# The selective scan of a hybrid decoder: running sums of the decays made once and spread through memory, one state without padding, outputs gathered chunk by chunk

## The reference

```python
a = dt * A                                  # per token and head, 32 heads in 8 groups of 4
a_cs = cumsum(a, within chunks of 128)      # 4 chunks
seg = a_cs[l] - a_cs[s]
Lmat = exp(where(l >= s, seg, -inf))
CB = C @ B.T                                # per group and chunk
y_diag = (CB * Lmat) @ X                    # X = x * dt, 64 features a head
chunk_states = B.T @ (exp(a_cs[-1] - a_cs) * X)
state = state * exp(a_cs[-1]) + chunk_states    # from chunk to chunk
y_off = (C @ state) * exp(a_cs)
y = (y_diag + y_off + d_skip * x) * silu(z)
y = y * rsqrt(mean(y * y within the group's 256 features) + eps) * norm_w
out = y @ w_out
```

## Time and profile before

| | us |
|---|---|
| median of 3 runs | 2250.75 (2249.43 to 2251.53) |
| the profiled execution | 2249.22 |
| its span | 2247.3 |
| TensorE busy in it | 2152.0 |
| VectorE busy | 1235.4 |
| ScalarE busy | 848.4 |

### The profile page before, as it was taken

One profiled execution on the slowest core, in us unless ns is written; L12 is line 12 of the kernel. 1 busy time (PEld: TensorE's weight loads), 2 busy tenths in 40 slices (PEclk: granted clock), 3 DMA queues, 4 the chain that ended last, 5 costly groups with the idle time before them and its releaser, 6 DMA issues. The chain is left out here.

```text
span 2247.3 us, 28900 instructions
## 1 busy us (share of the span) xinstructions
PE 2152.0 (96%) x10542; PEld 1807.0 (80%) x10542; DVE 1235.4 (55%) x2024; ACT 848.4 (38%) x1235; POOL 9.2 (0%) x30
## 2 busy tenths in 40 slices
PE   4999999899999999899999989999998899999998
PEld 2888888788888878788888878888887778888887
DVE  6555466778887763655556653333345765333323
ACT  4333322554445542422222344443134645322212
POOL 0000000000000000000000000000010000000000
PEclk8999999999999999999999999999999999999999
DMA  7555576112211113455547522223322012223231
GB/s 296 202 191 194 176 249 236 63 57 85 66 65 65 57 57 106 150 186 199 199 173 251 181 75 93 93 93 103 113 94 66 1 47 85 93 93 101 96 112 66
DMA packets 77528, 276.80 MB, mean 123 GB/s; under 512 B 8592, under 2 KB 11152, under 8 KB 77328
## 3 DMA queue, kind: packets, MB, share of 16 engines
q1 hardware_dynamic: 77456, 275.81, 35.7%
HBM read 273.68 MB, written 2.10 MB: 123 GB/s over the span
## 5 line engine op out<-in xcount | busy, mean ns | idle before, releaser
L236 PE MATMUL bank<-h_hi,w_hi_sb 128*128 128x512 f32 (+1 forms) x1984 | 757.6, 382 | 41.4 <-DVE h_lo L369 27.6
L237 PE MATMUL bank<-h_lo,w_hi_sb 128*128 128x512 f32 (+1 forms) x1984 | 749.0, 378 | 0.0
L238 PE MATMUL bank<-h_hi,w_lo_sb 128*128 128x512 f32 (+1 forms) x1984 | 748.5, 377 | 0.0
L231 DVE TENSOR_TENSOR w_lo_sb<-raw,w_hi_sb 128x1024 fp32r<-128x1024 f32 x356 | 419.9, 1197 | 124.9 <-ACT w_hi_sb L226 120.7
L236 PEld LDWEIGHTS bank<-h_hi,w_hi_sb 128*128 128x128 f32 x1984 | 376.1, 190 | 119.5 <-issue 21.5
L237 PEld LDWEIGHTS bank<-h_lo,w_hi_sb 128*128 128x128 f32 x1984 | 376.3, 190 | 69.0 <-issue 1.7
L238 PEld LDWEIGHTS bank<-h_hi,w_lo_sb 128*128 128x128 f32 x1984 | 376.1, 190 | 68.5
L226 ACT ACTIVATE w_hi_sb<-raw 128x1024 fp32r<-128x1024 f32 x356 | 352.7, 1031 | 86.7 <-PE bank L238 85.9
L236 PE MATMUL bank<-a_hi,w_hi_sb 128*128 128x512 f32 (+1 forms) x792 | 290.1, 366 | 0.0
L237 PE MATMUL bank<-a_lo,w_hi_sb 128*128 128x512 f32 (+1 forms) x792 | 289.4, 365 | 0.0
L238 PE MATMUL bank<-a_hi,w_lo_sb 128*128 128x512 f32 (+1 forms) x792 | 289.4, 365 | 0.0
(11 more groups left out here) (200 smaller groups left out, 1880.7 us busy)
## 6 DMA issues: line engine op xcount, KB each, us to landing
raw<-w_stream SPq DMA_DIRECT2D x356, 512.0 KB, 4.4
mod_raw<-w_mod SPq DMA_DIRECT2D x144, 512.0 KB, 4.4
first_mod<-w_mod SPq DMA_DIRECT2D x16, 512.0 KB, 14.5
x_trunk<-x_in SPq DMA_DIRECT2D x1, 2048.0 KB, 10.5
trunk_out<-x_trunk SPq DMA_DIRECT2D x2, 512.0 KB, 3.0
trunk_out<-x_trunk SPq DMA_DIRECT2D x4, 256.0 KB, 2.1
c_row<-c_in SPq DMA_DIRECT2D x1, 512.0 KB, 4.2
att_rows<-att_rows_in SPq DMA_DIRECT2D x1, 136.0 KB, 4.5
```

The lines of the kernel that those rows point to most:

```text
L231: nc.vector.tensor_tensor(w_lo_sb[:, s, 0:width], raw[:, s, 0:width], w_hi_sb[:, s, 0:width], ALU.subtract).then_inc(w_lo, 1)
L236: nc.tensor.matmul(ps, s_hi, m_hi, start=start, stop=False)
L237: nc.tensor.matmul(ps, s_hi, m_lo, start=False, stop=False)
L238: return nc.tensor.matmul(ps, s_lo, m_hi, start=False, stop=stop)
```

## The change

The running sums of all decays are made once, ahead of the first group, by two small products with triangles (`upto`, `from_mid`), turned on TensorE, and written to two tensors in memory: `sums_rows` as they are, `decay_rows` after Exp. ScalarE's queue then loads them for each group, spread over the partitions (`load_sums`, `load_decays`). ScalarE makes the decay between two tokens from them with a Relu for each head and one Exp for the chunk. Products with `after_r` and `ones_r` in the groups are gone, and with them `decays` on VectorE. The state is one tile without padding, multiplied by C alone; the decay is applied afterwards on VectorE, which gathers each chunk's output (`gather`) into `tmp`, to which ScalarE has written the skip term (`skip`). The sum of squares adds the two tiles on VectorE first, and takes one product with `ones`. The loops over pairs of groups are written out. In the last group four slabs of the output projection are used instead of two, in the order w_out 0, 2, 4, 6 of first halves, and then their second halves.

```diff
 def scan_a_tensor(pe, g, pp, c):
-            nc.tensor.transpose(bank[4][:, 2 * P:3 * P], bc[:, pp, 0, chunk[c]], ident[:, :])
+            if c < NCH - 1:
+                nc.tensor.transpose(bank[4][:, 2 * P:3 * P], bc[:, pp, 0, chunk[c]], ident[:, :])
             nc.tensor.matmul(cb, bc[:, pp, 0, chunk[c]], bc[:, pp, 1, chunk[c]], start=True, stop=True).then_inc(turned, 1)
-            pe.wait_ge(ta_ready, 4 * g + c + 1)
-            for n, (tri, ready) in enumerate(((after_r, seg_ready), (ones_r, sum_ready))):
-                for part in (ta_hi, ta_lo):
-                    mm = nc.tensor.matmul(bank[5 + n][:, :], tri[:, :], part[:, :, :].rearrange("p h l -> p (h l)"),
-                                          start=(part is ta_hi), stop=(part is ta_lo))
-                mm.then_inc(ready, 1)
+        def scan_b_tensor(pe, g, pp, c):
             pe.wait_ge(mixed, 4 * g + c + 1)
             if c:
                 pe.wait_ge(state_ready, 3 * g + c)
+                for pair in range(2):
+                    nc.tensor.matmul(bank[5][:, chunk[pair]], state[:, pair, :], bc[:, pp, 1, chunk[c]],
+                                     start=True, stop=True)
             for pair in range(2):
-                ps = bank[2 + pair][:, chunk[c]]
                 for r in range(2):
-                    mm = nc.tensor.matmul(ps, x_pad[:, r, pair, :], el[:, 2 * pair + r, :],
-                                          start=(r == 0), stop=(c == 0 and r == 1))
-                if c:
-                    for r in range(2):
-                        mm = nc.tensor.matmul(ps, state[:, r, pair, :], ee[:, 2 * pair + r, :],
-                                              start=False, stop=(r == 1))
+                    mm = nc.tensor.matmul(y_bank(c, pair), x_pad[:, r, pair, :], el[:, c % 2, 2 * pair + r, :],
+                                          start=(r == 0), stop=(r == 1))
...
 def ssm_tensor(pe):
+            def sum_decays(k):
+                if k == 4:
+                    pe.wait_ge(soft_dve, SOFT_A + 1)
+                    a = a_tok[:, :, :].rearrange("p c h -> p (c h)")
+                    nc.tensor.matmul(bank[5][:, 0:NCH * HEADS], after[:, :], a, start=True, stop=True)
+                    nc.tensor.matmul(bank[6][:, 0:P], upto[:, :], a, start=True, stop=True)
+                    pe.wait_ge(from_mid_ready, 1)
+                    nc.tensor.matmul(bank[6][:, P:2 * P], from_mid[:, :], a, start=True, stop=True).then_inc(dec_done, 1)
+            def turn_sums(k):
+                if k == 1:
+                    pe.wait_ge(acs_ready, 1)
+                    nc.tensor.transpose(bank[6][:, 2 * P:3 * P], acs[:, :], ident[:, :])
+                    nc.tensor.transpose(bank[6][:, 3 * P:4 * P], cd_all[:, :], ident[:, :]).then_inc(sums_turned, 1)
+                if k == 7:
+                    pe.wait_ge(ends_ready, 1)
+                    nc.tensor.matmul(bank[5][:, P:2 * P], ones[:, :], gm_t[:, :], start=True,
+                                     stop=True).then_inc(ends_spread, 1)
...
+                    if g == 0 and s < 2:
+                        pe.wait_ge(conv_step, 3 * (s + 1))
...
+                slab(0, sum_decays if g == 0 else None)
+                if g == 0:
+                    slab(1, turn_sums)
                 scan_a_tensor(pe, g, pp, 0)
-                slab(1)
+                if g:
+                    slab(1)
...
                 if not last:
                     slab(5)
-                for t in range(2):
-                    pe.wait_ge(gsq_ready, 2 * g + t + 1)
-                    mm = nc.tensor.matmul(bank[7][:, :], ones[:, :], zs[:, t, :], start=(t == 0), stop=(t == 1))
-                mm.then_inc(gstat_done, 1)
+                else:
+                    use_slab(pe, S_OUT // 4, 2, bank[4][:, :], y_hi, y_lo, 0, 8, 16)
+                pe.wait_ge(gsum_ready, g + 1)
+                nc.tensor.matmul(bank[7][:, :], ones[:, :], zs[:, 0, :], start=True, stop=True).then_inc(gstat_done, 1)
+                if last:
+                    use_slab(pe, S_OUT // 4, 3, bank[6][:, :], y_hi, y_lo, 0, 8, 16)
...
+        def load_sums(act, g):
+            act.dma_start(sums[:, :, :, :].rearrange("p c h l -> p c (h l)"),
+                          sums_rows[:, g, :].partition_broadcast(P)).then_inc(sums_loaded, 16)
+        def load_decays(act, g):
+            for r in range(2):
+                for c in range(1, NCH):
+                    act.dma_start(decays[r * HDIM:(r + 1) * HDIM, c - 1, :, :],
+                                  decay_rows[c, g, :, r, :].partition_broadcast(HDIM)).then_inc(decays_loaded, 16)
 def ssm_scalar(act):
+            act.wait_ge(sums_turned, 1)
+            nc.scalar.activation(tmp[:, 1, 0:P], bank[6][:, 2 * P:3 * P], ACT.Copy).then_inc(rows_ready, 1)
+            nc.scalar.activation(tmp[:, 1, P:2 * P], bank[6][:, 3 * P:4 * P], ACT.Exp).then_inc(rows_ready, 1)
+            act.wait_ge(rows_ready, 2)
+            act.dma_start(sums_rows.rearrange("c g (h l) -> (c g h) l", h=HPG), tmp[:, 1, 0:P]).then_inc(rows_stored, 16)
+            act.dma_start(decay_rows.rearrange("c g q r l -> (c g q r) l"), tmp[:, 1, P:2 * P]).then_inc(rows_stored, 16)
+            silu_tiles(act, 0, 0, range(4))
+            act.wait_ge(rows_stored, 32)
+            load_sums(act, 0)
+            load_decays(act, 0)
...
                 def scan(c):
+                    u = 4 * g + c
+                    if u > 1:
+                        act.wait_ge(y_done, u - 1)
+                    act.wait_ge(sums_loaded, 16 * (g + 1))
+                    for h in range(HPG):
+                        k = c * HEADS + HPG * g + h
+                        op = nc.scalar.activation(el[:, c % 2, h, :], sums[:, c, h, :], ACT.Relu, bias=acs[:, k:k + 1],
+                                                  scale=-1.0)
+                    op.then_inc(fall_ready, 1)
+                    act.wait_ge(fall_ready, u + 1)
+                    nc.scalar.activation(el[:, c % 2, :, :], el[:, c % 2, :, :], ACT.Exp, scale=-1.0).then_inc(el_ready, 1)
+                def skip():
+                    ...
+                    for t in range(2):
+                        nc.scalar.activation(tmp[:, t, :], xs[:, pp, t, :], ACT.Copy,
+                                             scale=ssm_cols[:, k:k + 1]).then_inc(xd_ready, 1)
...
+                if not last:
+                    act.wait_ge(el_ready, 4 * g + 4)
+                    load_sums(act, g + 1)
                 for t in range(2):
                     act.wait_ge(z_read, 2 * g + t + 1)
                     nc.scalar.activation(zs[:, t, :], zs[:, t, :], ACT.Silu).then_inc(silu_z, 1)
                 if not last:
                     silu_tiles(act, g + 1, 1 - pp, range(2))
-                for t in range(2):
-                    act.wait_ge(gate_step, 4 * g + 2 * t + 2)
-                    nc.scalar.activation(zs[:, t, :], tmp[:, t, :], ACT.Square).then_inc(gsq_ready, 1)
+                act.wait_ge(gate_ready, g + 1)
+                nc.scalar.activation(zs[:, :, :], tmp[:, :, :], ACT.Square).then_inc(gsq_ready, 1)
                 if not last:
+                    load_decays(act, g + 1)
                     conv_scalar(act, g + 1, 1 - pp, 3, used + 6, bank[1][:, :])
                     silu_tiles(act, g + 1, 1 - pp, range(2, 4))
...
 def ssm_vector(dve):
+                def gather(c):
+                    t = tmp[:, :, chunk[c]]
+                    if c == 0:
+                        dve.wait_ge(xd_ready, 2 * g + 2)
+                    dve.wait_ge(y_done, 4 * g + c + 1)
+                    nc.vector.tensor_tensor(t, t, y_bank(c), ALU.add).then_inc(y_step, 1)
+                    if c:
+                        d = decays[:, c - 1, :, :]
+                        dve.wait_ge(decays_loaded, 96 * (g + 1))
+                        nc.vector.tensor_tensor(d, d, bank[5][:, 0:2 * P].rearrange("p (q l) -> p q l", q=2),
+                                                ALU.mult).then_inc(y_step, 1)
+                        dve.wait_ge(y_step, 10 * g + 3 * c)
+                        nc.vector.tensor_tensor(t, t, d, ALU.add).then_inc(y_step, 1)
                 for s in range(6):
...
                     if 2 <= s <= 4:
                         carry(s - 2)
+                        gather(s - 2)
                     if 1 <= s <= 4:
                         mix(s - 1)
-                    if 1 <= s <= 3:
-                        decays(g, s)
...
+                gather(NCH - 1)
                 dve.wait_ge(silu_z, 2 * g + 2)
+                dve.wait_ge(y_step, 10 * g + 10)
+                nc.vector.tensor_tensor(tmp[:, :, :], tmp[:, :, :], zs[:, :, :], ALU.mult).then_inc(gate_ready, 1)
                 if not last:
                     conv_vector(dve, g + 1, 1 - pp, 3, bank[1])
-                    decays(g + 1, 0)
+                dve.wait_ge(gsq_ready, g + 1)
+                nc.vector.tensor_tensor(zs[:, 0, :], zs[:, 0, :], zs[:, 1, :], ALU.add).then_inc(gsum_ready, 1)
```

(107 more changed lines are left out.)

131 lines of the change are left out of this document (59 added, 72 removed).

## The result

The changed kernel takes 2269.68 us (median of 4 runs) against 2251.14: slower, ratio 1.0082, 95% interval 1.0064 to 1.0099. The forecast was 2262.6, range 2244 to 2274. The profiled execution takes 2268.54 us, its span is 2266.8; that is 19.5 more than before.

A forecast was written before the change was run, and what follows sets the result against it. TensorE, busy 96% of the span, was taken to bound the kernel. -48.3 saved, +56.7 for seven waits, +6.8 at the start and -3.3 at the end gave +11.9 on 2250.75: 2262.6 us, range 2244 to 2274.

The forecast's parts named there:

- What leaves TensorE: Scan and group ends: small products and passes dropped from TensorE's unbroken stream save 48.3 us, 6.0 a group.
- The seven waits: Ends of seven groups: TensorE waits for VectorE's addition, queued behind the last convolution; 56.7 us with clock.
- The size of the wait: At the ones product: 6.0 us each, 4.5 for the chain after slab 5 and 1.5 for ScalarE's DMA issues.
- The bound of 7.1: Upper bound in us of one wait at the ones product; the lower was 4.5.
- Rival (b): DMA issues on ScalarE cost nothing that shows, so the wait is 4.5 us and the kernel 2252; chance 17%.
- Clock: After each of the seven waits TensorE's clock falls to half rate for a while, costing 2.1 us a wait.
- The start: Before the first scan_b: the sums' round trip through memory puts it at 460.7; 6.8 us lost (5 to 9).
- The end: Last group: its wait at the statistics goes, only the one before the last scan_b stays; 3.3 us gained.
- Rival (d): VectorE, with 0.2 us margin, becomes the bound in the scan steps: about 10 us more, 2272; chance 13%.

The follow-up runs named there:

- six: Changed kernel with addition ahead of the last convolution, load_decays behind the skip copies (group 0 too), first sums in two DMAs, chunk 0 by itself: 2207.7 us.
- the second experiment: Changed kernel with only the six load_decays issues moved behind the next group's skip copies, instead of ahead of conv_scalar: 2246.8 us, ratio 0.9983.
- the third experiment: Changed kernel with 24 useless products on TensorE between slab 5 and the wait, in seven groups: 2254.1 us.
- the fourth: Kernel before, with only the squares added on VectorE behind the last convolution and one product with ones waiting for that: 2290.25 us, ratio 1.0186.

## Why the prediction was right

The direction, the place and the mechanism were right, and the size came out 6.6 us short: +11.9 forecast, +18.5 measured.

- **What leaves TensorE**: a chunk's step was forecast at 7.8 and is 7.79. That the saving is real shows in six: 42 of the 48.3 us are in the measured time. TensorE's waits from 405 to 960 us still sum to 21.5 us there, against 16.0 before, which is most of the rest.
- **The seven waits** were the cause. Moving the addition alone takes 29 us off, and the same wait put into the kernel before costs 40.
- **The size of the wait** is the term that was too small. I took 6.0 us, 4.5 for the chain and 1.5 for the issues; it is 6.6, and the second experiment parts it into 3.8 and 2.8. One of these issues takes 0.65 us, not the 0.45 worked out from SyncE's row. The queue alone doesn't make the difference: the 1 MB load is issued on ScalarE's queue too, in 0.38. The bound of 7.1 held. Rival (b), by which issues cost nothing, falls with the second experiment. The Trainium skill, DMA: Bandwidth & Descriptors, section Anatomy of one DMA, has about 50 ns for a sequencer's dispatch, given for GpSimd's path; the row here has 3.90 us for six, 13 times that.
- **Clock**: 2.1 us a wait assumed, 2.2 by the third experiment. With its 6.6, a wait costs 8.8 us, not 8.1; for all seven that is 46.1 + 15.6 - 56.7 = 5.0 us over the forecast.
- **The start** came out as worked out, `scan_b` at 461.2 against 460.7, but by errors that cancel. The load was issued at 447.8, not 450.6, while the first of the four Silu activations ahead of it in the order was only starting; and it took 9.4 us, not 6.5. By the Trainium skill's fit in the same section, made on GpSimd's path, a load of 1 MB takes an estimated 4.4 us; this broadcast doesn't follow it. The clock behind the wait cost more than the 2.1 us assumed: it is at its lower level until about 466.9, 5.7 us at half rate, so 2.8. In all the start costs 1.3 us more than forecast.

```profile
465.00:467.00 2.00, 2.00 (x6) 1.61 (x6) 1.97 (x7) 1.97 (x6) 0.00 (x0) 0.52 0.98 350
```

- **The end**: the wait at the statistics of the last group is gone, the one before the last `scan_b` is 2.6 us against 2.7. But the clock falls behind it, for 3.4 us, so 1.7 us are lost and not 0.6, and the end gains 2.3 us instead of 3.3.

```profile
842.00:844.00 2.00, 2.00 (x12) 1.98 (x12) 0.79 (x2) 0.00 (x0) 0.00 (x0) 0.59 0.28 16
844.00:846.00 2.00, 2.00 (x6) 1.51 (x5) 1.86 (x4) 0.00 (x0) 0.00 (x0) 0.55 0.64 238
```

- **Rival (d)** falls: no wait before a `scan_b` inside a group, though the margin was 0.2 us.
- **Open**: after the mixer, in the next feed-forward step, a wait for a slab is 3.85 us where the kernel before has 2.26. With the next one, right behind it, that is 4.7 against 3.5, 1.2 us of the difference. The two sum to 4.0 to 4.7 us in every experiment, also in the fourth with the old scan (4.1). It wasn't followed up, and its cause is open. Nor does the account close: 5.0 for the waits, 1.3 for the start, 1.0 for the end and 1.2 here make 8.5 us over the forecast, where the medians leave 6.6 and the two profiled executions 7.6, so 1 to 2 us of gain are in no term.

## What to carry to other kernels

When a reduction is moved from one engine to another to save a pass, look at what stands ahead of it in the new engine's order: here an addition of 0.7 us was queued behind work that itself needed the waiting engine's last product, and so a saving of 0.86 us a group became a wait of 6.6. The engine that bounds the kernel should not wait for something that is queued behind work on its own latest result. DMA issues on a compute engine's queue are work of that engine: put them where it is idle, and load first, by itself, the piece that is needed first.

## What the runs showed of the hardware

- A DMA issue on ScalarE's queue takes 0.65 us for 64 partitions of two pieces, 0.41 for the whole 1 MB load; these issues start beside a running activation, but the activation behind them in the order waits for them (2.89 us).
- A broadcast load of 1 MB lands 9.3 us after its issue (median of eight), one of 256 KB 3.8.
- Waits of 2.5 us, once a group, cost 1.2 us more than themselves on average, since the clock falls behind five of them and holds behind two; waits of 6.6 us cost 2.2 more.
- Filling the seven waits with useless products made the kernel 15.6 us faster.
